# Hybrid decoder trunk on one core: stages begin and end block by block, SSM outputs in groups of four

## What is computed

```
h = rmsnorm(x, ln1_g)
a_u, a_b, a_c, s_u, q, k, v, qi, ki, wi, gates = split_columns(h @ w_in)
y_a = (a_b * conv3(a_c * a_u)) @ w_out_a
y_b = s5(s_u) @ w_out_b      # 32 groups x 16 channels, 64 complex states, scan over tokens, GELU, GLU
y_c = dsa(q, k, v, qi, ki, wi) @ w_out_c   # indexer picks 64 keys per query, 8 heads
mixed = g0 * y_a + g1 * y_b + g2 * y_c     # g: sigmoid of gates, each of width 1024
x = x + mixed @ w_o
h2 = rmsnorm(x, ln2_g)
x = x + swiglu(h2, w1, w3, w2)             # layer 0: dense, 2816 hidden
x = x + moe(h2)                            # layer 1: top 2 of 8 experts, 3584 hidden each
```

## Time and profile before

| | us |
|---|---|
| three runs | 1762.76, 1767.69, 1764.49 |
| median | 1764.49 |
| profiled execution | 1763.59 |
| its span | 1761.8 |

### The profile page before, as it was taken

One profiled execution on the slowest core, in us unless ns is written; L12 is line 12 of the kernel. 1 busy time (PEld: TensorE's weight loads), 2 busy tenths in 40 slices (PEclk: granted clock), 3 DMA queues, 4 the chain that ended last, 5 costly groups with the idle time before them and its releaser, 6 DMA issues.

```text
span 1761.8 us, 24272 instructions
## 1 busy us (share of the span) xinstructions
PE 1687.8 (96%) x8960; PEld 1431.0 (81%) x8960; DVE 1369.3 (78%) x1135; ACT 1061.5 (60%) x860; POOL 427.0 (24%) x537
## 2 busy tenths in 40 slices
PE   7899998999979999979999999999999999999998
PEld 5887877999868878768888888888888888888886
DVE  6989575454459886558888888888888888888887
ACT  5443455544343544437777777777777777777775
POOL 8979400999024352020000000000000000000200
PEclk9999999999989999979999999999999999999999
DMA  9433365556443343638999999999999999999995
GB/s 326 122 118 116 125 203 176 178 192 200 152 156 121 117 149 129 206 119 293 389 358 388 370 378 386 370 369 382 371 373 378 375 374 389 362 382 369 385 395 193
DMA packets 212425, 481.53 MB, mean 273 GB/s; under 512 B 7904, under 2 KB 32608, under 8 KB 212112
## 3 DMA queue, kind: packets, MB, share of 16 engines
q1 hardware_dynamic: 207456, 463.34, 73.7%
q0 software_dynamic: 4480, 16.78, 2.6%
q10 hardware_dynamic: 432, 0.65, 0.1%
HBM read 473.40 MB, written 7.34 MB: 273 GB/s over the span
## 4 chain that ended last, share of the span: by engine, by line
PE 85%; DVE 10%; ACT 2%; issue 1%; DMA 1%; DVEq 0%; SPq 0%; ACTq 0%; POOLq 0%
PE ps L632 25%; PE ps L634 25%; PE ps L633 25%; DVE w_lo L277 3%; PE ps L1086 1%; PE ps L656 1%; PE ps L657 1%; PE ps L658 1%; ACT w_hi L272 1%; PE ps L755 1%; PE ps L780 1%; PE ps L698 1%; PE ps L782 1%; PE ps L757 1%; DMA raw<-w_in 1%
## 5 line engine op out<-in xcount | busy, mean ns | idle before, releaser
L277 DVE TENSOR_TENSOR w_lo<-raw,w_hi 128x2048 fp32r<-128x2048 f32 (+1 forms) x439 | 1012.1, 2313 | 271.0 <-ACT w_hi L272 269.8
L272 ACT ACTIVATE w_hi<-raw 128x2048 fp32r<-128x2048 f32 (+1 forms) x439 | 839.4, 1914 | 418.7 <-PE ps L634 399.8
L632 PE MATMUL ps<-w_hi,xg_hi 128*128 128x512 f32 x896 | 355.9, 397 | 1.8 <-issue 1.4
L634 PE MATMUL ps<-w_hi,xg_lo 128*128 128x512 f32 x896 | 350.2, 391 | 0.0
L633 PE MATMUL ps<-w_lo,xg_hi 128*128 128x512 f32 x896 | 349.7, 390 | 0.0
L632 PE MATMUL ps<-w_hi,hT_hi 128*128 128x256 f32 (+2 forms) x672 | 229.0, 341 | 2.2 <-DVE hT_lo L1627 2.2
L633 PE MATMUL ps<-w_lo,hT_hi 128*128 128x256 f32 (+2 forms) x672 | 225.3, 335 | 0.0
L634 PE MATMUL ps<-w_hi,hT_lo 128*128 128x256 f32 (+2 forms) x672 | 225.0, 335 | 0.0
L632 PE MATMUL ps<-w_hi,hidT_hi 128*128 128x512 f32 x536 | 209.7, 391 | 3.0 <-DVE hidT_lo L1949 3.0
L634 PE MATMUL ps<-w_hi,hidT_lo 128*128 128x512 f32 x536 | 208.8, 390 | 0.0
L633 PE MATMUL ps<-w_lo,hidT_hi 128*128 128x512 f32 x536 | 208.6, 389 | 0.0
(11 more groups left out here) (357 smaller groups left out, 2046.4 us busy)
## 6 DMA issues: line engine op xcount, KB each, us to landing
raw<-moe_w SPq DMA_DIRECT2D x336, 1024.0 KB, 7.2
raw<-w_in SPq DMA_DIRECT2D x44, 1024.0 KB, 5.5
raw<-ffn_w SPq DMA_DIRECT2D x33, 1024.0 KB, 5.2
raw<-w_o SPq DMA_DIRECT2D x8, 1024.0 KB, 4.9
raw<-w_out_a SPq DMA_DIRECT2D x4, 1024.0 KB, 4.9
raw<-w_out_c SPq DMA_DIRECT2D x4, 1024.0 KB, 5.0
raw<-w_out_b SPq DMA_DIRECT2D x4, 1024.0 KB, 4.9
raw<-w_in SPq DMA_DIRECT2D x4, 904.0 KB, 7.2
```

What stands on the lines that cost most here:

```text
L272: act.activation(w_hi[:, n % SPLIT, 0:width], raw[:, n % RAW, 0:width], ACT.Copy).then_inc(hi_done, 1)
L277: dve.tensor_tensor(w_lo[:, n % SPLIT, 0:width], raw[:, n % RAW, 0:width], w_hi[:, n % SPLIT, 0:width].bitcast(F32), ALU.subtract).then_in ...
L632: pe.matmul(dst, x_hi, hi, start=first, stop=False, skip_group_check=True)
L634: return pe.matmul(dst, x_lo, hi, start=False, stop=last, skip_group_check=True)
```

## The change

1. **Norm and turning by blocks.** Adding, squaring, scaling, transposing and the two parts are done for block 0 and then for block 1, in halves of 512 columns. A small ScalarE instruction loads the root's table ahead (`root_table`). The last two chunks before each norm run all of block 0 first (`two_rows`), the first chunk behind it runs block by block (`columns_block`, `rows_block`, `out_quarters`). The gain row of layer 1's first norm is loaded during mixer 0 into `su`, each gain on its own semaphore.
2. **SSM.** `bu` handles two steps at a time, on alternating row groups into banks 4 and 5; `y_of` handles four, on four column groups in turn. States of steps 2 to 5 lie in `uv`, which holds `u_t` and `v_t` otherwise. The value matmuls of attention alternate their column halves. `turn_q` and `add_skip` stand at other places in VectorE's list. The GLU chunk goes behind the first half of the last gate.
3. **Dense.** `up` holds the weights stationary and writes the hidden block turned; `turn_hidden` is gone. The hidden block of the last stripe has its own buffers `h_hi` and `h_lo`.
4. **First gather.** Token rows are picked with four matmuls of 512 columns for each half, copied, and transposed by four matmuls for each half. The second split of the experts stands behind the norm of the routing.

```diff
-BU_AT = (10, 12, 13, 14, 16, 17, 19, 20)
-Y_AT = (13, 14, 15, 17, 19, 20, 21, 22)
+QUAD = 4
+BU_AT = (10, 13, 18, 21)
+Y_AT = (17, 24)
...
+            def two_rows(n, xs, bank, parts, second_ready=None):
+                tile = lambda n, k, h: lambda w: slot_view(w, n, (2, D))[:, k, h * HALF:(h + 1) * HALF]
+                for i, (x_hi, x_lo, k0) in enumerate(xs):
+                    if i == 1 and second_ready is not None:
+                        pe.wait_ge(S["hidT_lo_done"], second_ready)
+                    pe.wait_ge(lo_done, n + i + 1)
+                    for k in range(2):
+                        for h in range(2):
+                            mm = three(ps[:, bank + h, :], x_hi[:, k0 + k, 0:P], x_lo[:, k0 + k, 0:P], n + i,
+                                       tile(n + i, k, h), False, i == 1 and k == 1)
+                mm.then_inc(parts, 1)
+                for h in range(2):
+                    for i, (x_hi, x_lo, k0) in enumerate(xs):
+                        for k in range(2):
+                            mm = three(ps[:, bank + 2 + h, :], x_hi[:, k0 + k, P:SEQ], x_lo[:, k0 + k, P:SEQ], n + i,
+                                       tile(n + i, k, h), False, i == 1 and k == 1)
+                        if h == 1:
+                            mm.then_inc(used, 1)
+                        elif i == 1:
+                            mm.then_inc(parts, 1)
...
+            def out_quarters(n, k0, x_hi, x_lo, layer):
+                pe.wait_ge(lo_done, n + 1)
+                for b in range(BLOCKS):
+                    tok = slice(b * P, b * P + P)
+                    for h in range(2):
+                        for k in range(2):
+                            mm = three(ps[:, 2 * b + h, :], x_hi[:, k0 + k, tok], x_lo[:, k0 + k, tok], n,
+                                       lambda w: slot_view(w, n, (2, D))[:, k, h * HALF:(h + 1) * HALF], False, k == 1)
+                        if (b, h) == (1, 1):
+                            mm.then_inc(used, 1)
+                        else:
+                            mm.then_inc(S["ob_quarters"], 1)
+                        if (b, h) == (1, 0):
+                            turn_block(mixed, 0, 4, S["mixed_done"], 5 * layer + 2, S["mixT_ps"])
...
+                qs = (2 * pair, 2 * pair + 1)
...
+                    c = 2 * (pair // 2) + jj
                     for part in range(2):
+                        for s, weights in ((0, ba[:, c, part, :]), (1, b_rows[:, c, part, :])):
+                            for q in qs:
+                                r = 32 * (q % 4)
+                                u2 = su[r:r + 32, c, :].rearrange("p (t s) -> p s t", s=HOP)
+                                dst = ps[:, 4 + q % 2, part * SEQ + jj * NCH:part * SEQ + (jj + 1) * NCH]
+                                mm = pe.matmul(dst, weights[r:r + 32, :], u2[:, s, :],
+                                               start=part == 0 and jj == 0 and s == 0, stop=s == 1,
+                                               skip_group_check=True, tile_position=(r, 0))
...
+                        for s in range(HOP):
+                            for q in range(QUAD * quad, QUAD * (quad + 1)):
+                                r = 32 * (q % 4)
+                                j = chunk_of(q, jj)
+                                dst = ps[r:r + 32, 5, jj * SEQ:(jj + 1) * SEQ].rearrange("p (t s) -> p s t", s=HOP)
+                                weights = (ca[:, part, 32 * j:32 * j + 32] if s == 0 else
+                                           par_sb[:, col + 32 * j:col + 32 * j + 32])
+                                mm = pe.matmul(dst[:, s, :], weights, state_at(q)[:, part, jj, s:s + NCH], start=False,
+                                               stop=s == 1 and part == 1, skip_group_check=True, tile_position=(0, r))
...
-                            for b in range(BLOCKS):
-                                tok = slice(b * P, b * P + P)
-                                mm = three(ps[:, bank, b * DENSE_W:(b + 1) * DENSE_W], hT_hi[:, k, tok],
-                                           hT_lo[:, k, tok], n,
-                                           lambda w: slot_view(w, n + which, (KD, DENSE_W))[:, k, :],
-                                           k == 0 and b == 0, k == KD - 1)
+                            for c in range(DENSE_W // P):
+                                dst = ps[:, bank, c * SEQ:(c + 1) * SEQ]
+                                cols = slice(c * P, (c + 1) * P)
+                                pe.matmul(dst, hi[:, k, cols], hT_hi[:, k, :], start=k == 0 and c == 0, stop=False,
+                                          skip_group_check=True)
+                                pe.matmul(dst, lo[:, k, cols], hT_hi[:, k, :], start=False, stop=False,
+                                          skip_group_check=True)
+                                mm = pe.matmul(dst, hi[:, k, cols], hT_lo[:, k, :], start=False, stop=k == KD - 1,
+                                               skip_group_check=True)
...
                 turn_q(0)
+                turn_q(1)
                 shift(layer, 1)
                 invert_sums(layer, 1)
                 chunk(13)
                 dve.wait_ge(S["v_made"], layer + 1)
                 conv(layer)
-                turn_q(1)
...
+                    pe.wait_ge(S["pick_done"], BLOCKS)
+                    for half in range(2):
+                        cols = slice(half * HALF, (half + 1) * HALF)
+                        for b in range(BLOCKS):
+                            for src in (h_hi, h_lo):
+                                mm = pe.matmul(ps[:, 2 + half, :], pick[:, b, :], src[:, b, cols],
+                                               start=b == 0 and src is h_hi, stop=b == 1 and src is h_lo,
+                                               skip_group_check=True)
+                        mm.then_inc(S["first_rows"], 1)
+                    for k in range(KD):
+                        if k % 4 == 0:
+                            pe.wait_ge(S["first_taken"], k // 4 + 1)
+                        tr = pe.transpose(ps[:, 6 + k // 4, (k % 4) * P:(k % 4) * P + P],
+                                          xg_tok[:, k * P:k * P + P], ident[:, :])
+                        if k % 4 == 3:
+                            tr.then_inc(S["gather_ps"], 1)
...
+            load_gain(2, flat(su[:, :, :]))
+            pool.wait_ge(S["x_added"], 4)
...
-            pool.wait_ge(S["x_added"], 4)
-            load_gain(2, gain_row)
```

More of the change, by code:

```diff
@@ L1624, in turned_lo, with add @@
[L1624 to L1628 removed]
+            def add(i, b, half, bank, after=None):
+                if (b, half) == (1, 1):
+                    dve.wait_ge(used, after)
+                else:
+                    dve.wait_ge(S["x_parts"], 2 * i - 1 + b)
+                part = x_tok[:, b, half * HALF:(half + 1) * HALF]
+                dve.tensor_tensor(part, part, ps[:, bank + 2 * b + half, :], ALU.add).then_inc(S["x_added"], 1)
@@ new lines, in scale @@
+            def scale(i, b, gains):
+                dve.wait_ge(S["std_done"], BLOCKS * i + b + 1)
+                own.then(dve.reciprocal(norm_ss[:, 5, b:b + 1], norm_ss[:, 4, b:b + 1]))
+                if b == 0:
+                    dve.wait_ge(S[f"gain_loaded{i}"], 16)
+                for half in range(2):
+                    cols = slice(half * HALF, (half + 1) * HALF)
+                    dve.scalar_tensor_tensor(h_tok[:, b, cols], x_tok[:, b, cols], norm_ss[:, 5, b:b + 1],
+                                             gains[:, cols], ALU.mult, ALU.mult).then_inc(S["h_done"], 1)
@@ new lines, in turned_lo, with enter @@
+            def turned_lo(i, b, ready, bank, done):
+                for half in range(2):
+                    dve.wait_ge(ready, 4 * i + 2 * b + half + 1)
+                    dve.tensor_tensor(turned_of(hT_lo, b, half), turned_ps(bank, b, half),
+                                      turned_of(hT_hi, b, half).bitcast(F32), ALU.subtract).then_inc(done, 1)
+            def enter(i, bank, after, gains, turned_bank):
+                add(i, 0, 0, bank)
+                add(i, 0, 1, bank)
+                variance(i, 0)
+                scale(i, 0, gains)
+                add(i, 1, 0, bank)
+                add(i, 1, 1, bank, after)
+                turned_lo(i, 0, S["hT_hi_done"], turned_bank, S["hT_lo_done"])
+                variance(i, 1)
+                scale(i, 1, gains)
+                turned_lo(i, 1, S["hT_hi_done"], turned_bank, S["hT_lo_done"])
@@ L2083, in stripe @@
                     lo(n0 + 9, turns)
[L2084 removed]
+                    times_up(this, w3_at, turned)
                 def y(e, y_used=None):
```

534 lines of the change are left out of this document (296 added, 238 removed).

## The result

The changed kernel takes 1749.8 us (median of 4 runs, 1748.7 to 1752.5), the kernel before 1764.1; the ratio is 0.992 (0.9905 to 0.993). It is faster by 14 us, where 34.9 were forecast, and lies above the range of 1719 to 1744. It is within 1 us of the time of the rival in which the quads don't run side by side. But that rival is wrong too: they do, and the loss is elsewhere.

The account below looks back on a forecast made before the run. TensorE, busy for 96% of the span, was taken as the bound, with VectorE setting the pace mid-mixer. Terms summed to 34.9 us: 1763.6 - 34.9 + 0.9 = 1729.6 us, range 1719 to 1744.

Parts of the forecast that it names:

- SSM, after chunk 17: Later mixer, TensorE the bound: inputs and outputs as pairs and quads save 6.5 us in layer 0, 6.8 in layer 1.
- SSM, before chunk 17: Earlier mixer, VectorE sets the pace: 0 gain in layer 0, 2.7 us of VectorE's wait saved in layer 1.
- Dense: Dense stretch: dropped transposes and the first wait for the hidden block save 5.3 us (bounds 4 and 6).
- End of dense and entry: Last up matmul to layer 1's second KV chunk: 31.5 us falls to 20.7, gain 10.8 (bounds 8 and 13).
- 4 cold: Block 1's half of layer 1's first KV chunk: 2.5 us at full clock, 4 at the lower clock.
- Output to W_O: Mixer output to W_O, merge behind a VectorE split: loss of 0.5 us in layer 0, 0 in layer 1.
- W_O to dense: Last W_O matmul to the up matmuls: block-wise entry saves 0.75 us (bounds 0 and 2.3).
- first gather: Picking token rows to the first expert matmul: 8.43 us falls to 6.1, gain 2.35 (bounds 0.5 and 4).
- the route before it: Routing: the experts' second split on VectorE ahead of low rows and logits loses 0.3 us (bounds -2.3 and 0.6).
- The first: Rival: VectorE bounds the whole mixer or TensorE's clock drops before chunk 16; mixers give 4 of 16, 1741 us; chance 0.13.
- The rival of the column groups: Rival: column groups don't run side by side, a quad costs 7.9 us, time 1750 us; chance 0.08.

Follow-up runs that it names:

- the last pair earlier: Changed kernel with GpSimd waiting for the convolution and the low hidden part made before the second split, plus last input pair behind chunk 20, not 21: 1732.2 us.

## Why the prediction was wrong

- **SSM, after chunk 17: the prices were right, the cover was not.** A quad measured 1.89 + 0.55 us (2.6 forecast), a pair 2.0 (2.0). So about 7 us of TensorE time did go (15.9 to 2 x 2.01 + 2 x 2.44 = 8.9). Layer 1 gave 5.5 of 6.8, and layer 0 2.1 of 6.5. The failed sentence is "VectorE has about 22 us of slack in those 72.50 and the rotation moves within it". The slack was a sum over the window. Pairs bunch the turns; turn 4 comes only behind chunk 20, and in layer 0 GpSimd then rotates and makes tables one after the other for turns 6 and 7. The run without these tables, on top of the last pair earlier, takes 75.7 us there, 6.7 less than with them and 8.0 under before.
- **SSM, before chunk 17: the step that cost most.** The failed sentences are "its list from turn_q(2) at 128.94 to the split of chunk 17 stays as long, and it waited only 1.51 us ahead of it. That part I put at 0 in layer 0." That length did hold, 25.8 us before and 26.2 after, to the end of that split. But turn 2 itself came 7.9 us later, and the wait ahead of it became 5.16. The list ahead of turn 2 wasn't looked at with the turn of step 1 in its new place, nor what GpSimd then does beside it. Layer 0 lost 8.3 us. The turn's place accounts for 5.2 of these (and 4.0 in layer 1), GpSimd beside the convolution for up to 7.1 (and 2.9); the two overlap. The run with the SSM part undone kept about 5 us of the loss, so a part of it comes with the other edits, whose effect on VectorE and the clock wasn't taken apart, and this part stays open.
- **Dense: the term was right, a wait took its place.** The transposes and the first wait were worth 5.3 us, and with the low part first the stretch is 178.0 us, 5.2 under before. As changed it gained 0.5: "I take 0" for the making of the halves was wrong by 4.7. The term had no place for the split ahead of the low part, which lasted 3.8 us and not 2.3 in the stripe that waited. In three other kernels this cost 3 us more. The up matmuls did keep their pitch of 0.12 us.
- **End of dense and entry: right** (11.4 for 10.8), and the gain row was worth 5.4 of it, 4.3 forecast. That the sum takes 4.2 us for the "4 cold" of the half chunk moves it by 0.2 only.
- **Output to W_O: sign right in layer 0, size low.** -2.4 and -0.8 for -0.5 and 0. The split ahead of the merge, which I named, held it; moving it is worth 2.6 to 4.1 us a layer. The same code gave 38.5 or 40.0 us in the runs, so 1.4 us of these two terms are no more than that.
- **Smaller terms:** W_O to dense 2.0 for 0.75, first gather 2.7 (8.43 to 776.77 - 771.02 = 5.75) for 2.35 and the route before it -1.0 for -0.3.
- **Rivals.** The first (VectorE the bound, clock falling ahead of chunk 16, 1741) named the mechanism and had 0.13, but it priced the loss at 12 us and it was 17.8 in the mixers, since it knew no loss below zero for the part before chunk 17. The rival of the column groups met the time by accident. The rule of the Trainium skill behind it, in TensorE: Matmul & The Clock Gate, section The mechanism, does not hold for column groups here: four matmuls that share all rows start within 10 ns of each other, and the weight loads of the next four start at 169.31, before those matmuls do at 169.41 and while the first four run.

## What to carry to other kernels

Take the list of the engine with slack instruction by instruction, not its busy share, before work is bunched: what matters is which instruction of it someone waits for, and what now stands ahead of it. Look at what a second elementwise engine will run at the same moment; making it wait was worth 11 us here. And where parts of a change are worth 5 to 10 us each, put each waited-for instruction first and time the parts alone: three moves of order and one added wait took this kernel from 1749.8 to 1725.1 us.

## What the runs showed of the hardware

The same twelve VectorE instructions took 10.7 us beside GpSimd's work and 5.0 without it, and a split of 128x2048 took up to 4.24 us beside it and never over 2.30 without it. Plain float32 matmuls of 128 rows by 32 columns of the array on four column groups in turn took 0.06 us each instead of 0.23, and even eight on one group and then eight on the next took 0.18.
